# Mixture-of-experts stage: the experts' tokens gathered from DRAM by an indirect DMA, and half of the scatter moved behind the next expert's first units

## The reference

```
logits = (t @ router).astype(jnp.float32)
top_logits, top_idx = lax.top_k(logits, TOP_K)
gates = jax.nn.softmax(top_logits, axis=-1)
combine = jnp.sum(jax.nn.one_hot(top_idx, N_EXPERTS, dtype=jnp.float32) * gates[..., None], axis=1)
for e in range(N_EXPERTS):
    out = out + combine[:, e:e + 1].astype(t.dtype) * swiglu(t, w_gate[e], w_up[e], w_down[e])
```

## Time and profile before

| | |
|---|---|
| median of 3 runs | 2727.1 us (2726.72 to 2729.7) |
| the profiled execution's own time | 2719.1 us |
| its span in the trace | 2717.3 us |
| PE busy | 2636.9 us (97%) |
| DVE, ACT, POOL busy | 1829.9, 1445.1, 29.6 us |
| DMA | 590.44 MB, mean 217 GB/s |

### The profile page before, as it was taken

How to read it: one execution, slowest core, us unless ns; L and a number is a source line. 1 busy time by engine, 2 the same in 40 slices (tenths; PEclk the granted TensorE clock), 3 DMA queues, 4 the chain that set the end, 5 groups by cost and what they waited for, 6 DMA issues and landing times.

```text
span 2717.3 us, 38945 instructions
## 1 busy us (share of the span) xinstructions
PE 2636.9 (97%) x15450; PEld 2214.3 (81%) x15450; DVE 1829.9 (67%) x1937; ACT 1445.1 (53%) x1599; POOL 29.6 (1%) x40
## 2 busy tenths in 40 slices
PE   7999999999998999998999999999999999999999
PEld 4875688888896999877799987788888888888887
DVE  4244665552535786774566554888888888888887
ACT  3235243332325555632344434877777777777776
POOL 0001000000002000000000000000000000000000
PEclk9999999999999999999999999999999999999999
DMA  8557312222330545320154532899999999999996
GB/s 356 209 209 278 125 63 100 102 93 85 109 141 34 192 170 184 127 93 2 63 186 150 190 148 78 323 358 354 342 372 344 365 349 366 348 363 350 342 371 256
DMA packets 84360, 590.44 MB, mean 217 GB/s; under 512 B 9616, under 2 KB 10000, under 8 KB 19472
## 3 DMA queue, kind: packets, MB, share of 16 engines
q1 hardware_dynamic: 82800, 576.79, 56.8%
q10 hardware_dynamic: 1440, 11.93, 1.1%
HBM read 587.63 MB, written 1.05 MB: 217 GB/s over the span
## 4 chain that ended last, share of the span: by engine, by line
PE 89%; DVE 6%; ACT 3%; DMA 1%; issue 1%; POOL 0%; DVEq 0%; SPq 0%; ACTq 0%; POOLq 0%
PE banks L471 24%; PE banks L473 24%; PE banks L472 24%; PE banks L477 14%; DMA ring<-in_stream 1%; PE banks L3038 1%; PE banks L989 1%; DVE ring_rounded L546 1%; ACT scratch L1066 0%; DVE rstd L894 0%; DVE aT L2370 0%; DVE activations L1507 0%; DVE nmax L1032 0%; DVE banks L1029 0%; ACT ring_rounded L536 0%
## 5 line engine op out<-in xcount | busy, mean ns | idle before, releaser
L472 PE MATMUL banks<-ring_rounded,activations_rounded 128*128 128x512 f32 x1344 | 523.2, 389 | 0.0
L473 PE MATMUL banks<-aT_rounded,ring_rounded 128*128 128x256 f32 (+2 forms) x1120 | 332.1, 297 | 0.0
L546 DVE TENSOR_TENSOR ring_rounded<-ring,ring_rounded 128x2048 fp32r<-128x2048 f32 (+4 forms) x112 | 225.3, 2017 | 147.2 <-ACT ring_rounded L536 146.3
L472 PEld LDWEIGHTS banks<-ring_rounded,activations_rounded 128*128 128x128 f32 x1344 | 252.7, 188 | 50.1
L472 PE MATMUL banks<-aT_rounded,ring_rounded 128*128 128x256 f32 (+1 forms) x856 | 283.7, 331 | 0.0
L536 ACT ACTIVATE ring_rounded<-ring 128x2048 fp32r<-128x2048 f32 (+4 forms) x112 | 188.5, 1690 | 150.9 <-PE banks L473 102.8
L3212 DVE TENSOR_TENSOR ring_rounded<-ring,tables_rounded 128x2048 fp32r<-128x2048 f32 x112 | 253.7, 2287 | 22.3 <-ACT tables_rounded L3130 21.7
L3212 DVE TENSOR_TENSOR ring_rounded<-ring,aT_rounded 128x2048 fp32r<-128x2048 f32 x112 | 254.4, 2286 | 15.4 <-ACT aT_rounded L3130 15.0
L3130 ACT ACTIVATE tables_rounded<-ring 128x2048 fp32r<-128x2048 f32 x112 | 215.1, 1920 | 85.5 <-DMA ring<-in_stream 73.6
L3130 ACT ACTIVATE aT_rounded<-ring 128x2048 fp32r<-128x2048 f32 x112 | 214.9, 1919 | 73.4 <-DMA ring<-in_stream 64.1
L473 PE MATMUL banks<-activations_rounded,ring_rounded 128*128 128x512 f32 (+1 forms) x724 | 245.4, 339 | 0.0
(11 more groups left out here) (362 smaller groups left out, 5603.8 us busy)
## 6 DMA issues: line engine op xcount, KB each, us to landing
ring<-in_stream SPq DMA_DIRECT2D x501, 1024.0 KB, 5.5
ring<-in_stream SPq DMA_DIRECT2D x32, 704.0 KB, 5.1
ring<-in_stream SPq DMA_DIRECT2D x28, 768.0 KB, 7.4
activations<-in_rpb ACTq DMA_DIRECT2D x2, 1536.0 KB, 6.3
ring<-in_stream SPq DMA_DIRECT2D x6, 512.0 KB, 5.1
tables<-in_tab_b ACTq DMA_DIRECT2D x1, 2436.0 KB, 8.4
tables<-in_tab_a ACTq DMA_DIRECT2D x1, 2304.0 KB, 13.4
hT<-in_h ACTq DMA_DIRECT2D x1, 2048.0 KB, 15.6
```

Source lines behind the costliest of these rows:

```text
L472: pe.matmul(out, exact(upper), exact(w_lower), start=False, stop=False)
L473: return pe.matmul(out, exact(lower), exact(w_upper), start=False, stop=stop)
L546: dve.tensor_tensor(exact(w), w, rounded(upper), ALU.subtract).then_inc(g.s["dve_pieces"], 1)
```

## The change

1. **The gather.** The tokens are stored once to a DRAM tensor `tokens` of 257 rows (two transfers of 128 rows from SP, and a row of zeros). In each expert PE makes, after the units of group i = 2, a one-column product of `perm` with `token_no` (token number minus 256; "listed"); DVE adds 256 and so has for each slot a row number, where an empty slot names the row of zeros. GpSimd, idle in this stage before, runs a loop of its own and issues an indirect DMA that brings the 128 rows into `by_slot`. PE turns them by 8 transposes, and that now stands behind `scatter(0)`, `scatter(1)` and ahead of the last three down units. ACT's and DVE's parts of `xg` move ahead accordingly (v = GU+4 and GU+5 of 2 GU).
2. **The scatter of columns 512 to 1023** is issued behind the first two units of the next expert, with `added(2)` and `added(3)` in that expert's first group. The first expert scatters zeros there (cleared by GpSimd); the last expert's half is scattered and added after the loop. Bank 7 takes the place of bank 3.
3. **Order on ACT and DVE**: the split of unit 46 now stands ahead of `result(1)`. Ahead of the loop the upper part of unit 0 moves in between the two token tiles of the routing, and the first gather's `xg` behind units 0 and 1, one half each.
4. **The tail**: gains and squares of the blocks k = 0 to 3 don't wait for the last scatter; PE's constant matmuls are 2, 2 and 3 in three places, where 6 stood in one.

```diff
@@ experts_pe
         def scatter(m):
-            bank = (0, 1, 6, 3)[m]
-            pe.wait_ge(s["dve_experts"], g.at("y lower", m // 2) + it * V)
+            if m < 2:
+                pe.wait_ge(s["dve_experts"], g.at("y lower", 0) + it * V)
+            else:
+                pe.wait_ge(s["dve_experts"], g.at("y lower", 1) - V + it * V)
...
                     unit(4 * i + 2 * n + h, bank, tokens(h), h == 0, h == 1)
+                if i == n == 0:
+                    for m in range(2, 4):
+                        scatter(m)
             if i >= 1:
                 transposes(i - 1)
+            if i == 2:
+                pe.wait_ge(s["dve_experts"], g.at("slots") + it * V)
+                for t in range(2):
+                    last = mm(pe, g.psum[7][:, 0:1], g.perm[:, t, :], g.token_no[:, t:t + 1], t == 0, t == 1)
...
         for m in range(2):
             scatter(m)
-        for v in range(GU + 4, 2 * GU):
-            down(v)
-        pe.wait_ge(s["dve_experts"], g.at("slots") + it * V)
+        pe.wait_ge(g.tokens_in, 16 + it * 16)
         pe.wait_ge(s["act_experts"], g.at("pwt") + it * A)
         for q in range(2):
             for j in range(4):
-                k = 4 * q + j
-                for t in range(2):
-                    last = mm(pe, g.psum[4 + q][:, P * j:P * j + P], g.t_tok[:, t, P * k:P * k + P],
-                              g.perm[:, t, :], t == 0, t == 1)
+                c = 512 * q + P * j
+                last = pe.transpose(g.psum[4 + q][:, P * j:P * j + P], g.by_slot[:, c:c + P], g.tab("ident"))
             last.then_inc(s["pe_experts"], 1)
-        for m in range(2, 4):
-            scatter(m)
+        for v in range(GU + 4, 2 * GU):
+            down(v)
@@ experts_act, the down half
         for v in range(2 * GU):
+            split(4 * GU + AHEAD + v)
             if v == 2 * GU - 1:
                 result(1)
-            split(4 * GU + AHEAD + v)
@@ experts_pool
+        pool.wait_ge(s["dve_experts"], g.at("slot list") + it * V)
+        pool.sem_inc(s["pool_listed"], 1)
+        pool.wait_ge(s["pe_experts"], g.at("gathered", 1) - Q + it * Q)
+        pool.sem_inc(s["pool_room"], 1)
+        pool.indirect_dma_start(g.by_slot, None, g.tokens,
+                                bass.IndirectOffsetOnAxis(ap=g.slot_list[:, 0:1], axis=0)).then_inc(g.tokens_in, 16)
@@ experts_sp
+    for t in range(2):
+        sp.wait_ge(s["act_routing"], g.at("free", ("by token", t, 1)))
+        sp.dma_start(g.tokens[P * t:P * t + P, :], g.t_tok[:, t, :]).then_inc(g.tokens_out, 16)
+    sp.wait_ge(s["pool_start"], 1)
+    sp.dma_start(g.tokens[L:L + 1, :], g.no_token[0:1, :]).then_inc(g.tokens_out, 16)
@@ store_pe
-    keep_warm(g, pe, 6)
+    warm(g, pe, g.psum[2], 2)
+    pe.wait_ge(*g.moment("experts over"))
+    for m in range(2, 4):
+        pe.wait_ge(*g.bank_free())
+        scatter_products(g, pe, m, g.open(("last added", m))).then_inc(g.s["pe_over"], 1)
+    keep_warm(g, pe, 2)
```

More of the change, by code:

```diff
@@ L2884, in route_pe, with first_upper_act @@
     keep_warm(g, pe, 3)
+def first_upper_act(g, act, n):
+    act.wait_ge(g.expert_in[n], 16)
+    act.activation(exact(g.upper[n]), g.units[n], ACT.Copy).then_inc(g.s["act_split"], 1)
 def route_act(g, act):
@@ L2975, in route_dve, with scatter_products @@
     dve.wait_ge(sem, g.so_far("dve_routing"))
+SCATTER_BANKS = (0, 1, 6, 7)
 def rounds_of(g, e):
     return e.value_load(g.rounds[0:1, 0:1], min_val=1, max_val=2)
+def scatter_products(g, pe, m, bank):
+    for j in range(2):
+        c = 256 * m + P * j
+        out = bank[:, L * j:L * j + L]
+        mm(pe, out, exact(g.yb[:, c:c + P]), exact(g.pwt[:, :]), True, False)
+        last = mm(pe, out, exact(g.yb_lower[:, c:c + P]), exact(g.pwt[:, :]), False, True)
+    return last
 def experts_pe(g, pe):
@@ L3108, in experts_act @@
     A, V, Q = g.per("act_experts"), g.per("dve_experts"), g.per("pe_experts")
[L3110 to L3117, removed]
+    first_upper_act(g, act, 1)
+    for q in range(2):
+        act.wait_ge(s["pe_first"], q + 1)
+        act.activation(exact(g.xg[:, 0, 4 * q:4 * q + 4, :].rearrange("p a b -> p (a b)")), g.psum[4 + q][:, :],
+                       ACT.Copy).then_inc(s["act_first"], 1)
+    for n in range(2, AHEAD):
+        first_upper_act(g, act, n)
+    act.wait_ge(s["pool_start"], 3)
     act.sem_inc(s["act_experts"], A)
@@ L3156, in experts_act @@
         for v in range(2 * GU):
+            split(4 * GU + AHEAD + v)
             if v == 2 * GU - 1:
                 result(1)
-            split(4 * GU + AHEAD + v)
+            if v == GU + 4:
+                for q in range(2):
+                    act.wait_ge(s["pe_experts"], g.at("gathered", q) + it * Q)
+                    act.activation(exact(g.xg[:, 0, 4 * q:4 * q + 4, :].rearrange("p a b -> p (a b)")),
+                                   g.psum[4 + q][:, :], ACT.Copy).then_inc(s["act_experts"], 1)
+                    g.count("act_experts", ("xg", q))
             if v == 0:
@@ L3170, in experts_act, with add_to_tokens @@
                 result(0)
[L3171 to L3175, removed]
     g.leave()
+def add_to_tokens(g, dve, m, bank):
+    h = g.hT[:, 2 * m:2 * m + 2, 0:L]
+    return dve.tensor_tensor(h, bank[:, :].rearrange("p (a b) -> p a b", a=2), h, ALU.add)
 def experts_dve(g, dve):
     s = g.s
-    rounds = rounds_of(g, dve)
     A, V, Q = g.per("act_experts"), g.per("dve_experts"), g.per("pe_experts")
@@ L3246, in experts_dve @@
             dve.wait_ge(s["dve_experts"], g.so_far("dve_experts") + it * V)
-            dve.wait_ge(s["pe_experts"], g.at("unit", 1) + it * Q)
+            dve.wait_ge(s["pe_experts"], g.at("listed") - Q + it * Q)
             for t in range(2):
@@ L3255, in experts_dve @@
                     split(4 * i + AHEAD + n)
+                if i == 0:
+                    added(2)
+                    added(3)
+                if i == 3:
+                    dve.wait_ge(s["pe_experts"], g.at("listed") + it * Q)
+                    dve.tensor_scalar(g.slot_list[:, :], g.psum[7][:, 0:1], float(L), None, ALU.add).then_inc(s["dve_experts"], 1)
+                    g.count("dve_experts", "slot list")
                 dve.wait_ge(s["pe_experts"], g.at("unit", 4 * i + 3) + it * Q)
@@ L3441, in second_block @@
     only("dve", experts_dve)
+    only("pool", experts_pool)
     if kind == "act":
-        squares_act(g, e, "last", g.hT, L, lambda k: "experts over")
-    only("dve", gain_dve)
+        squares_act(g, e, "last", g.hT, L, lambda k: "experts over" if k < 4 else ("added last", k // 2))
     only("pe", store_pe)
```

84 lines of the change are left out of this document (58 added, 26 removed).

## The result

The changed kernel takes 2732.84 us (median of 12 runs, 2727.5 to 2744.5), the kernel before, timed beside it, 2725.83 us (12 runs, 2720.1 to 2729.8). The ratio is 1.003, with a 95% interval of 1.0016 to 1.0045: slower by 0.3%, where 2713 us and a faster kernel were forecast. The profiled execution took 2732.7 us, its span is 2730.9 us. The span lies 27.6 us over the forecast and the median only 20: the forecast took over the 8 us by which the profiled execution of before lay under its median, and this one lies on its own.

A forecast was written before the change was run, and what follows sets the result against it. PE's instruction sum was taken to bound the kernel: start 1707.8, eight experts 972.2, waits 1.0, tail 22.3 gave a span of 2703.3, 14.0 under 2717.3. Taken off the median 2727.1, that gave 2713 us; 8-in-10 range 2708 to 2720.

The forecast's parts named there:

- The gather's other parts: Experts' loop: fetching the gathered rows stays hidden, ACT and DVE copy as before; 0 to 1.4 us an expert, taken as 0.
- the new place of `result(1)`: Behind the split of unit 46: "y lower" ready 5.1 us after that unit lands, against 5.45, a margin of 0.35 us.
- The forecast's own sign: Scatter to scatter in the loop: a period above 122.5 us would show the prediction wrong.
- the two that it named: Waits to blame if the period passed 122.5 us: the weights under ACT, or "y lower" under PE.
- An expert's work: PE's instructions per expert: 123.78 - 3.48 + 0.88 + 0.34 = 121.52 us, 2.26 less than before.
- Waits in the loop: PE waiting for "y lower" at the scatter behind the next expert's first two units: 1.0 us for all seven passes.
- rival 1: Passes between experts: the wait for "y lower" takes the gain; 2719 us, or 2730 at the longest landing; chance 0.13.
- the forecast's own rule: Landing of unit 46: each tenth of a microsecond over 5.35 is a tenth of a wait on PE.
- The start: Ahead of the loop: PE begins its first unit at 1707.8 instead of 1708.69.
- The tail: From PE's last unit to the end: 22.3 us, 1.7 of it half clock; no gain over 22.1 before.
- The gather's DMA and VectorE beside it: Experts' loop: the DMA's traffic and any DVE stall beside GpSimd stay within 5.0 us to spare; cost 0.
- Rival 2: Experts' stage: weights become the bound, 125.2 us an expert at 356 GB/s, 2742 us, slower; chance 0.06.

The follow-up runs named there:

- copies early: Changed kernel with ScalarE's two token copies and VectorE's two "xg lower" both ahead of the split of unit 44: 2716.0 us, ratio 0.996 to the kernel before.
- products, no DMA: Kernel with both token copies early, but the gather made by PE's 16 products from SBUF and no indirect DMA: 2732.6 us, ratio 1.0036.
- result(1) first: Kernel with both token copies early, plus result(1) ahead of the split of unit 46 on ScalarE and VectorE: 2711.7 us, ratio 0.9955.
- the start filled: Kernel with both copies early and result(1) first, plus three constant matmuls behind the first gather: 2710.8 us, ratio 0.9959.

## Why the prediction was wrong

**The step that failed** is one sentence of "The gather's other parts": "ACT and DVE do the same copies as before." The copies are the same, their place is not. Before, VectorE made "xg lower" ahead of the split of unit 46 and PE's scatter of the second half filled the time. Now that scatter comes later, so PE asks for the tokens directly behind unit 41, and "xg lower" stands behind the split of unit 45. The prediction weighed the new place of `result(1)` against landings to a tenth of a microsecond and never set the moment at which "xg lower" is ready against that at which PE asks. Its inputs were at hand: transposes done some 8 us ahead of unit 0, and from there on VectorE the splits of 43 to 45 (2.28 each), two additions (1.3) and "xg lower" (0.7 for the half that PE needs first) make 8.8, without any wait for a landing. Against 8.1 that alone is a wait of 0.7 us a pass. The rest of the measured 2.2 (1.2 to 3.15) is the landing of unit 44, on which that split hangs: with the median landing of 5.4 us, less the 3.9 found above, 1.5 us a pass or 10 in all. This is an estimate, and it leaves out the half clock behind the gaps.

**Point by point.** The span came out 27.6 us over the forecast 2703.3: 4.1 from the start, 23.3 from waits and the units behind them, and small differences. The forecast's own sign, a period above 122.5 us, came true (124.8 on the mean), but the wait was neither of the two that it named.
- An expert's work: forecast 121.52 us, measured 121.56 wherever no wait intervenes. So close a hit is in part luck: the gather was worth 0.11 us more than forecast, and the rest of the change cost 0.15 more.
- Waits in the loop: forecast 1.0 in all, for "y lower"; measured 15.5 for "xg lower" and 8.8 in the units behind, mostly half clock. The second part was no term of the loop's sum, though the forecast used one in the tail.
- "y lower": no wait in the changed kernel, but only since the other wait covered it; with the copies early it cost 2.5 us, between the forecast's 1.0 and rival 1. By the forecast's own rule its seven landings gave 1.5, not 1.0: 6.63 and 5.6 are 1.28 and 0.25 over 5.35.
- The start: forecast 1707.8, measured 1711.9. Kernels with the same code ahead of the loop began between 1708.0 (products, no DMA) and 1714.3 (both copies early), so a difference of 4 us is within what this part of the program varies by. PE's gap ahead of the first unit was 2.7 us where some 2.3 were forecast; the rest is that the first gather itself ended later, at 1709.1.
- The tail: forecast 22.3, measured 22.1, with a gap of 4.05 us and 4.52 us for 16 records behind it.
- The gather's DMA and VectorE beside it: forecast nothing, measured nothing (0.01 to 0.03 us an expert). The lock-out of which the Trainium skill warns (page "SBUF — State Buffer", section on the two separate sides) shows on one side: GpSimd waited for VectorE's splits in the 17 issues above. VectorE hardly ever waited for GpSimd: two splits of 2.34 and 2.35 us, begun 0.02 and 0.03 us ahead of an issue, are the only ones over 2.30 in the experts' stage of the eleven traces.
- Rival 2, the weights: didn't come. In the kernels with early copies the loop moves 44.6 MB in 121.56 us, gathered rows included, which is 367 GB/s. The Trainium skill (page "DMA: Bandwidth & Descriptors", section Bandwidth) ties its 358 to both cores of a pair streaming; here only one does, which the prediction didn't weigh.

With both copies early, result(1) first and the start filled, the profiled execution had its last unit's end at 2681.0 and a span of 2703.3 us, the two numbers of the forecast. That is luck in part: it was the fastest run (2705.1), with a first unit at 1708.0 where most traces have 1711.7 or more. The median is 2710.8 against 2724.3 of before, 13.5 us less (by the interval 7 to 15), where 14 were forecast. So the change can be worth about what the sum said, once the order is mended; the order of work that the change chose took that and more. The row is the first one behind the last unit:

```profile
2680.86 1.45 PE L477 MATMUL banks<-tables 128*128 128x384 f32 x4
```

## What to carry to other kernels

When a step is moved, ask at the new place for each of its consumers' inputs, not only for those of the step itself: removing the work that filled a dependency's latency turns "the same copies as before" into the critical path. Write down, for each wait of the engine that bounds the kernel, when the releaser finishes in its own queue and what stands ahead of it there; here the operation that PE waited for stood behind a split that had three units to spare, and putting it ahead of that split was worth some 15 us. Look again afterwards: the next wait, for "y lower", had been hidden behind the first. And count a gap of two microseconds or more on TensorE as more than its length: the seven longest of 14 gaps each cost 1.6 us again behind it, the three shortest nothing.

## What the runs showed of the hardware

- An indirect DMA of 128 rows of 4 KB, issued by GpSimd beside a stream at some 360 GB/s, takes 6.8 to 9.4 us to land in the changed kernel (5.9 to 12.3 in all eleven traces) and slows neither the stream nor VectorE measurably (124.27 us an expert without it, 124.28 with it). Its issue takes 0.94 us of GpSimd, but 2.3 to 3.1 where it began inside a split of VectorE with two inputs in SBUF (17 cases), and not where it began in VectorE's product of a PSUM bank and one input in SBUF.
- The half-clock stretch behind a short gap is one stretch of rows at 0.50 (2336.3 to 2339.7 above), then whole clock again; filling the gap with constant products removed it in 8 of 8 cases; left empty, gaps of 2.7 us ahead of the first expert were followed by it in six of eight kernels.
- Loads of one size, 1 MB, land in 4.9 to 8.8 us in the changed kernel's loop (median 5.5), so anything that stands behind one landing with less than 2 us to spare waits in some passes.
